# The gather of the next expert job inside the down products of this one, and the scatter of the last job inside the next first chunk, both in fp32r

## The reference, cut to what matters

```python
def moe_swiglu(h, w_router, b_router, w_gate, w_up, w_down):
    t = h.reshape(bsz * t_len, dm)
    logits = (t @ w_router) + b_router
    top_v, top_i = lax.top_k(logits, TOP_K)            # TOP_K = 2
    top_p = jax.nn.softmax(top_v, axis=-1)
    comb = jnp.sum(jax.nn.one_hot(top_i, N_EXPERTS) * top_p[..., None], axis=1)
    y = jnp.zeros_like(t)
    for e in range(N_EXPERTS):                          # 8 experts, 1024 -> 1408 -> 1024
        y = y + comb[:, e:e + 1] * swiglu(t, w_gate[e], w_up[e], w_down[e])
    return y
```

## Time and profile before

| what | value |
|---|---|
| median of 3 runs | 2067.61 us (2062.51 to 2070.7) |
| the profiled execution | 2062.35 us, its span 2060.5 us |
| TensorE busy in the span | 1839.1 us (89%) |
| VectorE, ScalarE, GpSimd busy | 1119.1 (54%), 869.2 (42%), 477.7 us (23%) |
| the expert loop, first product to the end of the last addition | 1480.67 to 2034.3 us |
| roundings of expert weights | 324, which is 9 jobs x 36 pieces |

### The profile page before, as it was taken

One profiled execution on the slowest core, in us unless ns is written; L12 is line 12 of the kernel. 1 busy time (PEld: TensorE's weight loads), 2 busy tenths in 40 slices (PEclk: granted clock), 3 DMA queues, 4 the chain that ended last, 5 costly groups with the idle time before them and its releaser, 6 DMA issues.

```text
span 2060.5 us, 40663 instructions
## 1 busy us (share of the span) xinstructions
PE 1839.1 (89%) x16512; PEld 1624.9 (79%) x16512; DVE 1119.1 (54%) x1609; ACT 869.2 (42%) x1273; POOL 477.7 (23%) x362
## 2 busy tenths in 40 slices
PE   4898878899989999979988789997799999999997
PEld 3796868787879999979887778787677877777775
DVE  0465575644232121035676774423588877788876
ACT  2435132142334433343532314233367665667654
POOL 0460000043345666636300004333000000000000
PEclk8899989999999999989999899999799999999998
DMA  9346454524233444424100003321788877788760
GB/s 310 91 133 206 140 183 136 163 87 128 93 113 115 131 124 125 146 72 127 59 3 5 2 5 101 115 92 55 250 293 306 277 256 263 273 300 311 258 236 31
DMA packets 225014, 314.76 MB, mean 153 GB/s; under 512 B 15585, under 2 KB 169575, under 8 KB 224743
## 3 DMA queue, kind: packets, MB, share of 16 engines
q1 hardware_dynamic: 217856, 306.22, 45.3%
q10 hardware_dynamic: 7014, 6.44, 1.1%
HBM read 310.53 MB, written 2.10 MB: 152 GB/s over the span
## 4 chain that ended last, share of the span: by engine, by line
PE 80%; DVE 12%; ACT 3%; issue 2%; DMA 2%; ACTq 1%; SPq 0%; DVEq 0%; POOL 0%
PE bank L562 77%; PE bank L559 2%; DMA ring<-in_w_ada 1%; DVE S L1666 1%; DVE cvT L1595 1%; DVE tmp L1610 1%; DVE hT L1462 1%; DVE rs L1457 1%; DVE U L1694 1%; DMA xin<-in_x_sample 0%; DVE hT L1469 0%; DVE xT L1488 0%; DVE e_w_rest L178 0%; DVE yT L1784 0%; DVE St L1712 0%
## 5 line engine op out<-in xcount | busy, mean ns | idle before, releaser
L1976 POOL TENSOR_TENSOR weights_rest<-ring,weights_rounded 128x512 fp32r<-128x512 f32 x344 | 463.1, 1348 | 627.0 <-ACT weights_rounded L1161 626.5
L178 DVE TENSOR_TENSOR e_w_rest<-e_raw,e_w_rounded 128x1024 fp32r<-128x1024 f32 (+1 forms) x324 | 351.5, 1130 | 46.2 <-ACT e_w_rounded L1398 37.9
L1161 ACT ACTIVATE weights_rounded<-ring 128x512 fp32r<-128x512 f32 x344 | 215.6, 629 | 378.1 <-PE bank L562 370.0
L1398 ACT ACTIVATE e_w_rounded<-e_raw 128x1024 fp32r<-128x1024 f32 (+1 forms) x324 | 312.5, 989 | 92.8 <-PE bank L562 86.7
L562 PE MATMUL bank<-h_rounded,weights_rounded 128*128 128x384 f32 x688 | 233.7, 340 | 31.4 <-DVE h_rest L1503 31.4
L562 PE MATMUL bank<-h_rest,weights_rounded 128*128 128x384 f32 x688 | 232.7, 338 | 0.0
L562 PE MATMUL bank<-h_rounded,weights_rest 128*128 128x384 f32 x688 | 232.6, 338 | 0.0
L562 PE MATMUL bank<-e_w_rounded,hG_rounded 128*128 128x512 f32 (+1 forms) x432 | 163.8, 379 | 15.3 <-DVE hG_rest L1934 14.3
L562 PE MATMUL bank<-e_w_rounded,hG_rest 128*128 128x512 f32 (+1 forms) x432 | 161.4, 374 | 0.0
L562 PE MATMUL bank<-e_w_rest,hG_rounded 128*128 128x512 f32 (+1 forms) x432 | 161.1, 373 | 0.0
L562 PEld LDWEIGHTS bank<-h_rounded,weights_rounded 128*128 128x128 f32 x688 | 131.5, 191 | 33.9 <-issue 33.1
(11 more groups left out here) (280 smaller groups left out, 3451.8 us busy)
## 6 DMA issues: line engine op xcount, KB each, us to landing
ring<-in_w_ada SPq DMA_DIRECT2D x96, 512.0 KB, 5.6
e_raw<-in_moe_w_down SPq DMA_DIRECT2D x90, 512.0 KB, 5.2
ring<-in_w_in SPq DMA_DIRECT2D x88, 512.0 KB, 4.7
e_raw<-in_moe_w_gate SPq DMA_DIRECT2D x72, 512.0 KB, 6.1
e_raw<-in_moe_w_up SPq DMA_DIRECT2D x72, 512.0 KB, 7.2
e_raw<-in_moe_w_gate SPq DMA_DIRECT2D x36, 384.0 KB, 5.7
e_raw<-in_moe_w_up SPq DMA_DIRECT2D x36, 384.0 KB, 3.9
ring<-in_ffn_w_gate SPq DMA_DIRECT2D x22, 512.0 KB, 4.8
```

The costliest lines, as they stand in the source:

```text
L178: eng.tensor_tensor(wl, e_raw[n % E_RAW][:, 0:kn * w], wr.bitcast(F32), ALU.subtract).then_inc(s("e_rest"), 1)
L1161: a(w_parts[n % NSLOT][0], raw, ACT.Copy).then_inc(*E.up("rounded_ready", *key))
L1398: a(e_w[n % E_PARTS][0][:, 0:kn * w], e_raw[n % E_RAW][:, 0:kn * w], ACT.Copy).then_inc(s("e_rounded"), 1)
L1976: pool.tensor_tensor(wl, raw, wr.bitcast(F32), ALU.subtract).then_inc(*E.up("rest_ready", *key))
```

## The change

- Gather: the 384 tokens are kept as rounded part and rest (`hT_parts`, `htoken` in the order); ScalarE and VectorE make these once, behind the router. The gather of a job is now two runs of 24 fp32r products, one with the rounded part (into banks 2 and 3), one with the rest (banks 0 and 1). The sums are copied by ScalarE straight to the two parts of `hG`, so that VectorE's subtraction goes. For job i + 1 they stand behind pieces 29 and 32 of job i (`GATHER_AT`); for the first job in front of the loop.
- Scatter: `ey` is rounded part and rest, and the scatter is two fp32r products per output instead of one in fp32. That of job i - 1 stands in job i's first chunk, one output behind each of pieces 2 to 7; the last job's stands behind the loop. The first job scatters zeros.
- Weights of the tokens: they no longer sit in `selc`. `wsel` holds them; three products of one column bring them into the job's order (`wslot`), and `ey` is scaled by them as it is copied. `sel` itself is turned into `selT`, in front of the second chunk (`slots`).
- Selection of the next job: behind the second chunk instead of the end of the job on VectorE.

The diff, cut to what the sections below speak of:

```diff
@@ tensor engine @@
-                pe.wait_ge(s("e_sel"), i + 1)
-                pe.wait_ge(s("e_ydrained"), i * 2 + 2)
-                for j in range(3):
-                    last = transpose(psum[4][:, j * P:(j + 1) * P], selc[:, j, :])
...
-                        last = mm(psum[6 + k // 4][:, (k % 4) * P:(k % 4 + 1) * P], htok[:, j, k * P:(k + 1) * P],
-                                  sel[:, j, :], j == 0, j == 2)
...
+            def gather(part):
+                for k in range(KD):
+                    b = psum[2 - 2 * part + k // 4]
+                    for j in range(3):
+                        last = mm(b[:, (k % 4) * P:(k % 4 + 1) * P], hT_parts[part][:, j, k * P:(k + 1) * P], sel[:, j, :], j == 0, j == 2)
+                    if k % 4 == 3:
+                        last.then_inc(s("e_gather"), 1)
+
+            def slots(i):
+                for j in range(3):
+                    transpose(psum[4][:, j * P:(j + 1) * P], sel[:, j, :].bitcast(F32))
+                for j in range(3):
+                    last = mm(psum[5][:, 0:1], sel[:, j, :].bitcast(F32), wsel[:, j:j + 1], j == 0, j == 2)
+                last.then_inc(s("e_selT_full"), 1)
+
+            def scatter(i, n_):
+                j, half = divmod(n_, 2)
+                if n_ == 0:
+                    pe.wait_ge(s("e_ey"), i * 2 + 2)
+                if n_ >= 2:
+                    pe.wait_ge(s("e_sc_done"), i * 6 + n_ - 1)
+                cols_ = slice(half * 512, (half + 1) * 512)
+                mm(psum[6 + half][:, :], selT[:, j, :], ey[0][:, cols_], True, False)
+                mm(psum[6 + half][:, :], selT[:, j, :], ey[1][:, cols_], False, True).then_inc(s("e_sc"), 1)
...
+                    if c == 1:
+                        slots(i)
...
+                        if 2 <= n < 8:
+                            scatter(i, n - 2)
...
+                    if n == GATHER_AT[0]:
+                        pe.wait_ge(s("e_sel"), i + 2)
+                        gather(0)
+                    elif n == GATHER_AT[1]:
+                        gather(1)
+            for n_ in range(6):
+                scatter(njobs, n_)
@@ scalar engine @@
+            def e_gathered(i, part):
+                for h in range(2):
+                    act.wait_ge(s("e_gather"), i * 4 + 2 * part + h + 1)
+                    a(hG[part][:, 4 * h:4 * h + 4, :], psum[2 - 2 * part + h][:, :].rearrange("p (k s) -> p k s", k=4), ACT.Copy)\
+                        .then_inc(s("e_hG"), 1)
+            e_gathered(0, 0)
+            e_gathered(0, 1)
...
                 act.wait_ge(s("e_used"), i * NPC + E_PARTS + NPC)
                 for half in range(2):
-                    a(ey[:, half * 512:(half + 1) * 512], psum[4 + half][:, :], ACT.Copy).then_inc(s("e_ydrained"), 1)
+                    a(ey[0][:, half * 512:(half + 1) * 512], psum[4 + half][:, :], ACT.Copy, scale=wslot).then_inc(s("e_eyr"), 1)
@@ vector engine @@
+            for k in range(6):
+                dve.wait_ge(*at("htok_rounded", k))
+                hi, lo = (p_.rearrange("p j d -> p (j d)")[:, k * 512:(k + 1) * 512] for p_ in hT_parts)
+                tt(lo, bank("htok", k)[:, :], hi.bitcast(F32), SUB).then_inc(*E.read("htok", k))
...
+            for zero in (ey[0], ey[1], selT):
+                dve.memset(zero.bitcast(F32), 0.0).then_inc(*E.step())
...
+            def add_output(i, n_):
+                j, half = divmod(n_, 2)
+                dve.wait_ge(s("e_sc"), i * 6 + n_ + 1)
+                dst = yacc[:, j, half * 512:(half + 1) * 512]
+                tt(dst, dst, psum[6 + half][:, :], A).then_inc(s("e_sc_done"), 1)
+
+            def output_rest(i):
+                for half in range(2):
+                    dve.wait_ge(s("e_eyr"), i * 2 + half + 1)
+                    cols_ = slice(half * 512, (half + 1) * 512)
+                    stt(ey[1][:, cols_], psum[4 + half][:, :], wslot, ey[0][:, cols_].bitcast(F32), M, SUB).then_inc(s("e_ey"), 1)
...
+                done = E_PARTS - 1
+                e_rests(0, done)
+                output_rest(i)
...
+                    if c == 0:
+                        for n_ in range(6):
+                            e_rests(done, 5 + n_)
+                            done = 5 + n_
+                            add_output(i, n_)
...
+                    if c == 1:
+                        dve.wait_ge(s("e_selT_full"), i + 1)
+                        select(dve.value_load(rt_i[0:1, bass.ds(i + 19, 1)], min_val=0, max_val=NCODE - 1)).then_inc(s("e_sel"), 1)
```

More of the change, by code:

```diff
@@ L29 @@
 DOWN = ((0, 4), (4, 4), (8, 3))
+GATHER_AT = (29, 32)
 E_PIECES = [(which, 2 * k, 2, c0, n) for c0, n in CHUNKS for which in ("moe_w_gate", "moe_w_up") for k in range(KD // 2)]
@@ L1020, in _ @@
-                last.then_inc(s("e_selT_full"), 1)
-                pe.wait_ge(s("e_sc_done"), i * 6 + 6)
-                for k in range(KD):
-                    for j in range(3):
-                        last = mm(psum[6 + k // 4][:, (k % 4) * P:(k % 4 + 1) * P], htok[:, j, k * P:(k + 1) * P],
-                                  sel[:, j, :], j == 0, j == 2)
-                    if k % 4 == 3:
-                        last.then_inc(s("e_gather"), 1)
-                pe.wait_ge(s("e_hG_rest"), i * 2 + 2 + 2)
+                pe.wait_ge(s("e_hG"), i * 4 + 4)
@@ L1046, in _ @@
                     e_piece(i, n, eprodT, lambda k, c0: (psum[4 + (E_PIECES[n][3] + c0) // 512], k == 0, k == KE - 1))
-                pe.wait_ge(s("e_ydrained"), i * 2 + 2 + 2)
-                for j in range(3):
-                    for half in range(2):
-                        n_ = 2 * j + half
-                        if n_ >= 2:
-                            pe.wait_ge(s("e_sc_done"), i * 6 + 6 + n_ - 1)
-                        mm(psum[6 + half][:, :], selT[:, j, :], ey[:, half * 512:(half + 1) * 512], True, True)\
-                            .then_inc(s("e_sc"), 1)
+                    if n == GATHER_AT[0]:
+                        pe.wait_ge(s("e_sel"), i + 2)
+                        gather(0)
+                    elif n == GATHER_AT[1]:
+                        gather(1)
+            for n_ in range(6):
+                scatter(njobs, n_)
             for m in range(4):
@@ L1899, in _ @@
             dve.tensor_copy(rt_i[:, 17:34], jl).then_inc(*E.up("jobs_ready"))
-            for k in range(6):
-                dve.wait_ge(*drained('htok', k))
             s = lambda name: sem(name).h
             dve.memset(yacc, 0.0).then_inc(*E.step())
+            for zero in (ey[0], ey[1], selT):
+                dve.memset(zero.bitcast(F32), 0.0).then_inc(*E.step())
+            dve.memset(wslot, 0.0).then_inc(*E.step())
             dve.wait_ge(*E.latest())
             dve.sem_inc(s("e_prod"), 3)
-            dve.sem_inc(s("e_sc_done"), 6)
-            dve.sem_inc(s("e_hG_rest"), 2)
+            dve.sem_inc(s("e_eyr"), 2)
             njobs = dve.value_load(rt_i[0:1, 0:1], min_val=NE, max_val=NJOB)
@@ L1949, in _ @@
                 e_rests(done + 4, NPC)
-                select(dve.value_load(rt_i[0:1, bass.ds(i + 19, 1)], min_val=0, max_val=NCODE - 1)).then_inc(s("e_sel"), 1)
-                for n_ in range(6):
-                    j, half = divmod(n_, 2)
-                    dve.wait_ge(s("e_sc"), i * 6 + 6 + n_ + 1)
-                    if n_ == 0:
-                        dve.wait_ge(s("e_sc_done"), i * 6 + 6)
-                    dst = yacc[:, j, half * 512:(half + 1) * 512]
-                    tt(dst, dst, psum[6 + half][:, :], A).then_inc(s("e_sc_done"), 1)
+            output_rest(njobs)
+            for n_ in range(6):
+                add_output(njobs, n_)
             dve.tensor_copy(stat[:, 84:85], ident[:, 0:1]).then_inc(*E.up("yacc_ready"))
```

58 lines of the change are left out of this document (26 added, 32 removed).

## The result

The changed kernel takes 2095.32 us in the median of 4 runs (2093.14 to 2098.07); the kernel before, run beside it, 2065.11. The ratio is 1.0135, 95% interval 1.0109 to 1.0161: 1.35% slower (28 us), with the whole interval above 1. The prediction was 2076.5 (2048 to 2092), so the measured time lies outside the range. The profiled execution has a span of 2092.7 us against 2060.5.

The account below looks back on a forecast made before the run. TensorE, busy 89% of the span, was taken as the bound. Jobs of 61.5 us against 62.35 give -6.8; entry +5.2, last job +10.5 and tail -0.3 make +8.6, say +9: 2076.5 us, range 2048 to 2092.

Parts of the forecast that it names:

- the turn that stays: Between jobs, TensorE waits for ScalarE's two result copies, rounding of piece 0 and its rest: 3.8 us per job.
- entry: Before the loop: later rests, more memsets, gather, then the first rounding bare; first product at 1485.9 instead of 1480.67, +5.2 us.
- eight periods: Expert loop: a job takes 61.5 us against 62.35, 0.85 gained per job, eight times, 6.8 us.
- last job and tail: End of loop: unneeded gather, slots and selection still run, +10.5 us; tail 7.6 against 7.9, -0.3.
- The gather at 0.113: Inside each job: 48 fp32r products of 128 columns at the fp32 gather's beat, 5.4 us per job.
- the slots: In front of the second chunk: 3 transposes and 3 one-column fp32 products, 9 records, 1.0 us per job.
- the scatter: In the first chunk: 12 fp32r products of 512 columns at 0.229, 2.7 us per job.
- A: Gather: narrow fp32r runs as fp32 does, two records' worth, 5.4 us more per job, 2133 us; chance 0.15.
- B: Gather: narrow fp32r goes by its columns, 0.062 per product, 2.4 us less per job, 2052 us; chance 0.08.
- The selection: VectorE, behind the second chunk: three comparisons and three tiny copies that no slack covers, 0.95 us added per job.
- Rival C: VectorE becomes the bound; each microsecond per job gives +9 us, at 1.2 it is 2087; chance 0.05.
- it takes 8.1 as before: First gather, before the loop: takes 8.1 us as in the kernel before, starting at 1474.0 instead of 1471.0.

Follow-up runs that it names:

- e1_warm_turn: Changed kernel plus 14 unused 512-column filler products at the head of every job, where TensorE otherwise idles; 2079.43 us, ratio 1.0076 to the kernel before.
- e2: Changed kernel with its two gather runs behind pieces 27 and 29 instead of 29 and 32; 2092.61 us, ratio 1.0156 to the kernel before.
- e9: Changed kernel with 6 unused 512-column filler products at the head of each job, leaving about 2.3 us idle; 2077.2 us in one run.
- e7: Changed kernel whose gather products multiply only 64 of the 128 columns of sel, with the same number of products; 2092.99 us in one run.
- e6_all: e4 plus the selection between the rests of pieces 15 and 16 and gather behind pieces 28 and 31; 2038.03 us, ratio 0.9876 to the kernel before.
- e10: e6_all with 46 unused 512-column filler products ahead of the first job's gather; 2040.12 us in one run.
- e4: Changed kernel with ScalarE rounding the next job's first three pieces ahead of its two result copies; 2049.94 us, ratio 0.9946 to the kernel before.
- e11: e10 with 37 fillers and three clearings moved to VectorE's wait for the router's logits; 2028.39 us, ratio 0.9822 to the kernel before.
- e13: e11 with 18 fillers ahead of the first gather instead of 37, and three more behind it; 2028.78 us, ratio 0.9831 to the kernel before.
- e8: Changed kernel with both gather runs in plain float32 instead of fp32r, two records per product; 2129.09 us in one run.
- e12: Changed kernel with 30 narrow 128-column fp32r filler products in the turn; 2077.92 us in one run.
- e3: Changed kernel with VectorE's selection between the rests of pieces 15 and 16, not behind the second chunk; 2084.34 us, ratio 1.0113 to the kernel before.

## Why the prediction was wrong

**The failed step** is "the turn that stays", taken as 3.8 us of waiting and nothing more. The waiting was right to 0.1 (3.73 measured). What it left out is the clock: the view of a job before showed 1.00, and I carried that over, though the change takes away just the scatter and gather that had kept TensorE busy in the turn. Before, the longest wait in the turn was 1.58 (the load and product at 1605.34 waited so long for the gathered rest); now there is one of 3.7 us, and the granted clock falls in it or just behind it every time. Priced by e1_warm_turn this is 2.07 us per job: 16.7 in eight periods (in the first of them it is the half clock brought along from the entry, in the other seven that of a turn) and 1.5 more in the last job (67.4 against e1's 65.9). The Trainium skill warns of it ("TensorE: Matmul & The Clock Gate", "HAM oscillation — how this bites in real kernels"): gaps in TensorE's work put the clock back to 1.2 GHz and the work behind them pays. The traces agree (0.50 behind the idle time), and it should have stood among the rivals. The same page ("What's actually happening") says that the same kernel can see more or fewer slow products from run to run; what the traces show is such a spread inside one execution, from turn to turn (6.8 or 3.4 us at half clock in the changed kernel, none in some turns of e2 and e9).

**By steps.** Counted from the router's last group to the last addition the kernel gets 27.8 us longer, where the sum gave 8.6:

| part | predicted | measured | difference |
|---|---|---|---|
| entry | +5.2 | +7.9 | 2.7 |
| eight periods | -6.8 | +7.6 | 14.4 |
| last job and tail | +10.2 | +12.3 | 2.1 |

The periods: without the clock (e1) they are 61.2, so the sum per job was 0.3 too high and the clock is all of the miss (8 x 2.07 = 16.6, less 8 x 0.3 = 2.4). The prediction had named a period over 63 as a sign of being wrong. The gather at 0.113 (0.110 measured), the slots (1.0 predicted, 0.92 measured) and the scatter (2.7 and 2.8) stand; rivals A and B, which lived on another price of a narrow product, fall, and e7 shows why B did: columns don't count there. The selection: predicted 0.95, measured 0.77. That the wait of "about 1.2" was met (1.20) is in part luck: the prediction counted it from 0.27 before the change, where the row that shows 1.20 now had 0.43. Rival C falls: there are no waits for VectorE in the first chunk, and e6_all brings a job to 56.7 us without VectorE becoming the bound.

The entry: the gather begins 3.65 later instead of 3.0 (the 0.65 stays open), and "it takes 8.1 as before" was wrong for the same reason as the turn, a clock taken over: 10.5, because narrow fp32r products leave it at 0.50 where fp32 ones raised it. e10 shows 5.4 at full clock.

The last job and tail: the clock's 1.5 us, and the tail itself, 7.6 predicted, is 8.5.

**What the change is.** Its idea is worth something: with the turn closed (e4), the same moves make the kernel 0.5% faster than before, with the selection moved as well and the gather one piece earlier (e6) 1.2%, and with the entry put in order (e11, e13) about 1.7 to 1.8%. What made it 1.35% slower is in the 27.8 us above: 20.6 are added time at half clock (16.7 in the periods, 1.5 in the last job, 2.4 in the gather at the entry). The other 7.2 are near the 8.6 of the sum: eight periods gain 9.1, and that does not pay for what is added once, 5.5 at the entry and 10.8 in the last job with its tail, where gather, slots and selection run for a job that doesn't exist. The moved work had covered ScalarE's copies and the first rounding, in their written order; the wait so bared was in the sum, the clock behind it was not.

## What to carry to other kernels

When work leaves a stretch in which the busiest engine waits, price the wait twice: its length, and the clock that may fall in it and stay down for some us behind it; a window's clock of 1.00 before the change says nothing of the stretch that the change bares. A filler of useless products in the gap is a quick test of that second price. Then look at what else was covered by the moved work, here the order of copies and roundings on ScalarE: closing the wait at its source paid 5.1 us per job, the filler 2.1. And count what is paid once, at the entry and in the last pass of the loop: here it ate the whole gain of the periods.

## What the runs showed of the hardware

- A stream of 48 narrow fp32r products left the clock at 0.50 for 10.5 us; 48 records of plain fp32 at the same starts, 0.22 apart, brought it to 1.00 after 4.7 (e8), and wide fp32r products after 3.3 (e10; also e11 and e13, and 5.3 in e1 behind the narrow gather). Yet narrow fp32r products held a full clock through a turn (e12).
- The clock fell in all turns with 3.7 us of idle time in the changed kernel, e3, e7 and e8 (32 of 32; between 2.0 and 5.2 us behind the last product, so at times only inside the next job), in six of eight in e2, in two of eight with 2.3 (e9), in none with 0.9 (e4), and once behind narrow products and 0.86 us of idle time (e11), where e10 kept it. What decides a single case stays open.
- A fall left the clock down for 3.4 us in some turns and 6.8 in others of the same execution, at 1.45 and some 2.55 us of time.
- A narrow fp32r product cost 0.110 us at full clock, the same at 64 and 128 columns, and 0.22 at half clock.
- The place in time of one and the same early product differs by up to 14 us between profiled executions, so spans of single executions have to be aligned at a point behind which the kernels differ.
